# Gate rows of a two-block transformer kernel: summed over partitions on GpSimd instead of TensorE and VectorE

## The chip, the cores and the metric

The kernel runs on one core of a Trainium2 chip. The metric is device time of one execution in microseconds (us). The engines are called as the profile calls them: PE (TensorE, matrix products; PEld is its weight load), DVE (VectorE), ACT (ScalarE), POOL (GpSimd), SP (SyncE, which issues most DMAs). SBUF is the working memory of 128 partitions, PSUM the eight banks that PE writes.

## What is computed

Two transformer blocks run one after the other on 256 tokens of width 1024, in float32. The parts that matter here:

```python
# modulation, from a conditioning vector c of 1024 values
mod  = silu(c)   @ w_ada[l]   + b_ada[l]      # first block: 6 vectors of 1024 (sh1, sc1, gt1, sh2, sc2, gt2)
ada  = silu(c_2) @ w_ada_2[l] + b_ada_2[l]    # second block: 9 vectors of 1024
# first block
x = x + gt1 * mix(x, ctx)                                            # gate 0
x = x + gt2 * swiglu(modulate(rmsnorm(x), sh2, sc2), w_ffn_in, w_ffn_out)   # gate 1
x = rmsnorm(x, g_final)
# second block
x = x + 0.5 * g1 * swiglu(modulate(rmsnorm(x), sh1, sc1), ...)       # gate 2
x = x + g2 * (merged @ w_out)                                        # gate 3
x = x + 0.5 * g3 * swiglu(modulate(rmsnorm(x), sh3, sc3), ...)       # gate 4
x = rmsnorm(x, final_norm)
```

A gate is one vector of 1024 that multiplies every token's update. There are five of them. A swiglu is `(silu(h @ Wa) * (h @ Wb)) @ Wout` with inner width 2816.

## The kernel before

**Products in three parts.** Each weight tile of 1 MB (128 x 2048 floats, a "unit") is loaded by SP into one of three `raw` buffers. ACT rounds it to a high half (`whi`, line 862), DVE subtracts to get the low half (`wlo`, line 1912, a DVE operation with two SBUF inputs), and PE forms high x high, high x low and low x high (line 1291). PE may start a unit when its low half is ready (`lo_ready`). The activations have high and low halves in the same way: `A_both`, `B_hi`, `B_lo`.

**Stages.** The order on each engine is written out by hand, and engines meet only at semaphores. The stages are: the first block's mixer (units `P1`, from `dd` and `k` to `gla_out` and `mix_out`), `ffn(0)`, `ffn(1)`, the second block's mixer (`P2`, ending in `bra`, `brb`, `out2`), `ffn(2)`. Between them stands a norm. A feed-forward block has 11 pieces of 256 inner columns. Step i does two "up" units and one "down" unit. A step of PE waits for the DVE product of the piece before (`prod_done`) and its down product waits for `B_lo` (`flo_done`). `feed_forward_steps` (line 465) runs the steps, partly as a hardware loop of three steps a turn.

**Modulation.** The vectors `silu(c) @ w_ada` are not formed on PE. A unit of modulation is 256 columns: 1 MB of weights lands in `ada_raw`, and DVE adds eight products of a column block with a scalar per partition into `acc` (lines 1916 and 1920). After that each partition holds a part of the sum, and the sum over the 128 partitions is still to be taken. `GATE_UNITS` are the first of the four units of each gate. Gate r becomes a row `GR`, the same 1024 values in every partition, as follows:
- POOL loads the bias row into `GR` (`gate_bias`, line 716);
- PE multiplies a matrix of ones with `acc`, which sums over partitions and repeats the result in all of them (`gate`, line 1363): two products of 128x512, which in float32 are two passes each;
- DVE adds the two PSUM banks to `GR` (`gate_row`, line 1982).

Gate 0 is formed ahead of `mix_out`, gates 1, 2 and 4 ahead of the last down unit of the three feed-forward blocks, gate 3 ahead of `out2`. DVE then multiplies results with `GR`.

**POOL** otherwise issues the loads of modulation weights in the mixers (`load_ada`, line 776), computes the powers for the norms (`split_norm`, `piece_norm`, `twice_norm`), and turns a bias table around for the second block's attention (line 833). It works strictly in the order of its program.

**Modulation units of the last block.** Units 48 to 51, gate 4's, are loaded and summed in steps 0, 7, 8 and 9 of `ffn(2)` (`LAST_STEPS`). In `ffn(0)` and `ffn(1)` there is one such unit in every step from 0 to 9.

Of the kernel before, what the change touches and what calls it, by code (L numbers as in the profile page):

```python
# [15 lines left out]
P = 128  # L16
# [106 lines left out]
ADA_FFN = [n for n in range(len(ADA)) if NADA1 <= n < ADA_P2 or n >= ADA_LAST]  # L123
ADA_MIX = [n for n in range(len(ADA)) if n not in ADA_FFN]

LAST_STEPS = (0, NF - 4, NF - 3, NF - 2)


def ada_pos(n):
# [17 lines left out]
def build(nc, a, out):  # L147
    with ExitStack() as ctx:
# [3 lines left out]
        def sem(name):  # L152
            return ctx.enter_context(nc.semaphore(name))
# [182 lines left out]
        as_rows = sem("as_rows")  # L336
        as_turn = sem("as_turn")
        as_done = sem("as_done")
        gr_mm = sem("gr_mm")
        gr_done = sem("gr_done")  # L340
        x_ready = sem("x_ready")
        sq_done = sem("sq_done")
# [121 lines left out]

        def feed_forward_steps(eng, f, step):

            end = NF - 1 if f < 2 else NF - 4
            with eng.Fori(0, (end - 1) // 3) as j:
                for m in range(1, 4):
                    step((j, m), m)  # L470
            for i in range(end, NF - 1):
                step(i, i)


        def cview(w, c0, n=UC):
# [164 lines left out]

            return 7 if n in (3, 4) else 3

        def gate_bank(r):

            return {0: 6, 3: 2}.get(r, 4)

        def h_count(n, k):

# [54 lines left out]
        def _(pool):  # L703
# [12 lines left out]
            def gate_bias(r):  # L716
                blk, c0 = ADA[GATE_UNITS[r]]
                b = a["b_ada"] if blk == 0 else a["b_ada_2"]
                pool.dma_start(GR, b[0, c0:c0 + D].partition_broadcast(P)).then_inc(gr_in, 16)

            def negative_root(dst, src):

# [98 lines left out]
            for n in range(7, NADA1):  # L821
                load_ada(n)
                if n == 8:
                    pool.wait_ge(on_done, 8)
                    gate_bias(0)
            split_norm(2)
            gate_bias(1)
            twice_norm()
            gate_bias(2)
            pool.wait_ge(u_in, 16)  # L830
# [4 lines left out]
            for f in range(HR):  # L835
                ins = nc.gpsimd.memset(inv[:, f:f + 1], float(10000.0 ** (-2.0 * f / ROPE)))
            ins.then_inc(inv_done, 1)
            piece_norm(1, 8, rstd_done)
            gate_bias(3)
            load_ada(ADA_P2)  # L840
            for j, w in ((0, QR), (1, KVR)):
                pool.wait_ge(act_evac, EV2[j][1])
                root(rs2[:, 2 * j:2 * j + 2], ss2[:, 2 * j:2 * j + 2], w).then_inc(lat_rs, 1)
            for n in range(ADA_P2, ADA_LAST):
                if n > ADA_P2:
                    load_ada(n)
            split_norm(5)
            gate_bias(4)
            piece_norm(2, 14, frs_done)


# [437 lines left out]
        def _(pe):  # L1289
# [70 lines left out]
                            ins.then_inc(tr_done, 1)  # L1360
                keep_warm(warm, 3)

            def gate(r):

                g0 = GATE_UNITS[r]
                pe.wait_ge(*ada_done(g0 + 3))
                pe.wait_ge(gr_in, 16 * (r + 1))
                for x in range(2):
                    c = UC * ada_pos(g0) + 512 * x
                    ins = mm(bank[gate_bank(r) + x][:], ones[:], acc[:, c:c + 512], True, True)  # L1370
                ins.then_inc(gr_mm, 1)

            def shift_and_scale(n, b):

                pe.wait_ge(*ada_done(NORM_UNITS[n][1] + 3))
# [158 lines left out]
            def ffn(f):  # L1534
                u0, n0 = BASE_FFN[f], NF * f

                def up_step(u, b, half, k):

                    s = ring(u)
                    ws = slice(P * half, P * half + P)  # L1540
                    wh = whi[s][:].rearrange("p (k w) -> p k w", k=KD)[:, k, ws]
                    wl = wlo[s][:].rearrange("p (k w) -> p k w", k=KD)[:, k, ws]
                    o = bank[b + half]
                    pair = A_both[:, k, :, :].rearrange("p s t -> p (s t)")
                    if k:
                        mm(o[:, 0:T], wl, A_hi[:, k, :], False, False, skip_group_check=True)
                        return mm(o[:], wh, pair, False, k == KD - 1, skip_group_check=True)
                    mm(o[:], wh, pair, True, False, skip_group_check=True)
                    return mm(o[:, 0:T], wl, A_hi[:, k, :], False, False, skip_group_check=True)

                def up(u, i, b):

                    pe.wait_ge(lo_ready, lin(3, i, u + 1))
                    for half in range(2):
                        for k in range(KD):
                            ins = up_step(u, b, half, k)
                    ins.then_inc(unit_used, 1)

                def first_up(u, b, before):

                    for k in range(KD):
                        pe.wait_ge(hlo_done, before + k + 1)
                        for half in range(2):
                            ins = up_step(u, b, half, k)
                    ins.then_inc(unit_used, 1)

                def down(u, i, m, first, last):

                    pe.wait_ge(lo_ready, lin(3, i, u + 1))
                    pe.wait_ge(flo_done, lin(1, i, n0 + 1))  # L1570
                    s = ring(u)
                    wh = whi[s][:].rearrange("p (k w) -> p k w", k=2)
                    wl = wlo[s][:].rearrange("p (k w) -> p k w", k=2)
                    for t in range(TT):
                        for x in range(2):
                            for k in range(2):
                                ts, cs = slice(P * t, P * t + P), slice(512 * x, 512 * x + 512)
                                kb = 2 * (m % 3) + k
                                ins = three(bank[2 * t + x][:], (wh[:, k, cs], wl[:, k, cs]),
                                            (B_hi[:, kb, ts], B_lo[:, kb, ts]), False,  # L1580
                                            first and k == 0, last and k == 1, skip_group_check=True)
                            if last and 2 * t + x < 3:
                                ins.then_inc(bank_down, 1)
                    ins.then_inc(unit_used, 1)

                def step(i, m):
                    pe.wait_ge(prod_done, lin(1, i, n0 + 1))
                    up(u0 + 2, i, 4)
                    up(u0 + 3, i, 6)
                    down(u0 + 4, i, m, False, False)  # L1590


                pe.wait_ge(lo_ready, u0 + 1)
                first_up(u0, 0, low_count(2 + f + (f == 2)))
                up(u0 + 1, 0, 2)
                up(u0 + 2, 0, 4)
                up(u0 + 3, 0, 6)
                pe.wait_ge(prod_done, n0 + 1)
                down(u0 + 4, 0, 0, True, False)
                feed_forward_steps(pe, f, step)  # L1600
                pe.wait_ge(prod_done, n0 + NF)
                gate((1, 2, 4)[f])
                down(u0 + 2, NF - 1, NF - 1, False, True)

            def second():
# [52 lines left out]
                for n2, (kind, n) in enumerate(P2):  # L1658
                    u = BASE_P2 + n2
                    b = BANKS2[n2]  # L1660
                    s = ring(u)
                    if (kind, n) == ("out2", 0):
                        gate(3)
                    pe.wait_ge(lo_ready, u + 1)
                    wait_banks(n2, BEFORE2[n2][:1] if (kind, n) == ("bra", 0) else BEFORE2[n2], EV2)
                    if kind in ("uq", "ukv"):
# [190 lines left out]
            for u, (kind, n) in enumerate(P1):  # L1857
                if u < 2:
                    continue
                b = BANKS1[u]  # L1860
                if kind == "mix_out" and n == 0:
                    gate(0)
                pe.wait_ge(lo_ready, u + 1)
                wait_banks(u, BEFORE1[u], EV1)
                x = B if kind in ("conv_out", "gla_out") else A
# [37 lines left out]
        def _(dve):  # L1903
# [64 lines left out]
            def columns(n, b, gain, bias0, src):  # L1968
# [9 lines left out]
                    link(tt(by4(scale[:, s, :]), sums[:, 1], by4(bcol[:, bias0 + KD:bias0 + 2 * KD]), ALU.add))  # L1978
                    ins = stt(scale[:, s, :], scale[:, s, :], 1.0, vec[:, gain:gain + KD], ALU.add, ALU.mult)
                ins.then_inc(as_done, 1)  # L1980

            def gate_row(r):
                dve.wait_ge(gr_mm, r + 1)
                for x in range(2):
                    g = GR[:, 512 * x:512 * x + 512]
                    ins = tt(g, g, bank[gate_bank(r) + x][:], ALU.add)
                ins.then_inc(gr_done, 1)

            def norm(n):
                src, dst = (ctxX if n == 0 else xg if n == 3 else X), norm_source(n)  # L1990
# [314 lines left out]
            def ffn(f):  # L2305
# [41 lines left out]
                product(NF - 1, 4)  # L2347
                split(u0 + 3 * NF)
                low(NF - 1, NF - 1)
                r = (1, 2, 4)[f]  # L2350
                gate_row(r)
                dve.wait_ge(gr_done, r + 1)
                if f != 1:
                    dve.wait_ge(fin_in, 16 * (f // 2 + 1))
                for t in range(TT):
# [34 lines left out]
            def second():  # L2390
# [126 lines left out]
                for n2 in range(N2):  # L2517
# [31 lines left out]
                    if n2 in ADA2_STEP:  # L2549
                        adapt_half(ADA_P2 + ADA2_STEP.index(n2))  # L2550
                    if P2[n2] == ("out2", 0):
                        gate_row(3)
                        dve.wait_ge(gr_done, 4)
                evac2(N2 - 1)

# [11 lines left out]
            for u in range(N1):  # L2567
                if u:
                    evac1(u - 1)

                gla_step(2 * (u - 1 - U_Q) + 1)
                if u and u != U_V:
                    split(u + 2)
                gla_front(u)
                gla_step(2 * (u - U_Q))
                if u in (U_Q + 1, U_Q + 2):
                    decayed_queries(u - U_Q - 1)
                if P1[u - 1][0] == "ch":
                    conv(P1[u - 1][1])
                if P1[u - 2][0] == "ch":  # L2580
                    conv_low(P1[u - 2][1])
                if u == U_CB + 8:
                    norm_heads()
                if u in MOD_STEP:
                    n = MOD_STEP[u]
                    adapt(n, 0, acc[:, UC * ada_pos(n):UC * ada_pos(n) + UC], ADA[n][0])
                if P1[u] == ("mix_out", 0):
                    gate_row(0)
                    dve.wait_ge(gr_done, 1)
            evac1(N1 - 1)  # L2590
            norm(2)
# [59 lines left out]
```

## Time and profile before

| | |
|---|---|
| median of 3 runs | 1157.66 us (1157.28 to 1157.92) |
| span of the profiled execution | 1156.4 us |
| PE busy | 1118.4 us, 97% |
| DVE busy | 853.4 us, 74% |
| ACT busy | 571.7 us, 49% |
| POOL busy | 74.7 us, 6% |
| mean granted clock of PE | 0.991 |

The span runs from the first to the last instruction; the measured time is 1.26 us longer than it. In the rows, L1912 is line 1912 of the kernel, a shape `128x2048` is partitions x elements, and `arena` is one large SBUF tensor that holds most intermediate tiles, so `acc` and `GR` appear as `arena` and PSUM banks as `twin`. Times are us unless marked ns. A PE pass is recorded longer than the distance at which passes follow each other.

### The profile page before, as it was taken

What the parts mean: (1) busy time and instruction counts of PE and PEld (TensorE: products, weight loads), DVE (VectorE), ACT (ScalarE), POOL (GpSimd) and SP (SyncE); (2) the same over time, 40 slices, a digit from 0 to 9 for tenths busy, and PEclk for the clock granted to TensorE, in tenths of its full rate; (3) what the DMA queues carried; (4) which work ended last, traced back from release to release, by engine and by line L of the source; (5) the groups of instructions that cost most, each with busy time, mean ns of one, the idle gap of its engine ahead of it and who ended that gap; (6) DMA issues with size and microseconds to landing.
All of it is one profiled execution on the core that took longest, in us unless ns stands there. A gap on an engine that the chain in (4) does not pass through costs nothing.

```text
span 1156.4 us, 19131 instructions
## 1 busy us (share of the span) xinstructions
PE 1118.4 (97%) x7744; PEld 1008.5 (87%) x7744; DVE 853.4 (74%) x1082; ACT 571.7 (49%) x733; POOL 74.7 (6%) x143
## 2 busy tenths in 40 slices
PE   2999999999999999999999999999999999999997
PEld 2899988999999888888788888889999998888885
DVE  1578766897777688877888778878777776755676
ACT  3495434544434644445454454446655546444442
POOL 4000000100000100000200000011000001000001
PEclk8899999999999999999999999999999999999999
DMA  9934554688875488778468777747965654655771
GB/s 287 291 114 140 188 175 154 183 273 263 296 233 187 154 282 272 238 247 293 154 226 271 252 258 263 239 152 240 292 183 182 222 178 165 218 182 191 234 247 37
DMA packets 192548, 250.29 MB, mean 216 GB/s; under 512 B 4859, under 2 KB 171966, under 8 KB 192350
## 3 DMA queue, kind: packets, MB, share of 16 engines
q1 hardware_dynamic: 183838, 216.92, 57.8%
q0 software_dynamic: 8640, 32.38, 8.4%
q8 instruction: 51, 0.84, 0.3%
q14 instruction: 19, 0.16, 0.0%
HBM read 248.23 MB, written 1.05 MB: 216 GB/s over the span
## 4 chain that ended last, share of the span: by engine, by line
PE 87%; DVE 7%; ACT 2%; SPq 2%; DMA 1%; issue 1%; POOL 0%; POOLq 0%; DVEq 0%; ACTq 0%
PE twin L1291 85%; DVE wlo L1912 2%; DVE arena L1920 2%; DMA arena<-in_w_ada 1%; DVE arena L1912 1%; ACT arena L862 1%; DVE X L1912 1%; ACT whi L862 1%; PE twin L1628 1%; SPq L520 1%; SPq L570 0%; DVE arena L1916 0%; PE twin L1749 0%; PE twin L1416 0%; DVE B_lo L1912 0%
## 5 line engine op out<-in xcount | busy, mean ns | idle before, releaser
L1291 PE MATMUL twin<-A_both,whi 128*128 128x256 f32 (+1 forms) x2208 | 578.7, 339 | 3.1 <-DVE A_both L1912 1.6
L1912 DVE TENSOR_TENSOR wlo<-raw,whi 128x2048 fp32r<-128x2048 f32 (+1 forms) x171 | 386.9, 2263 | 117.1 <-ACT whi L862 117.0
L1291 PE MATMUL twin<-A_both,wlo 128*128 128x256 f32 x1632 | 436.5, 280 | 0.0
L862 ACT ACTIVATE whi<-raw 128x2048 fp32r<-128x2048 f32 x169 | 323.2, 1913 | 206.8 <-PE twin L1291 205.7
L1291 PEld LDWEIGHTS twin<-A_both,whi 128*128 128x128 f32 x2208 | 370.1, 190 | 46.1 <-issue 7.9
L1291 PEld LDWEIGHTS twin<-A_both,wlo 128*128 128x128 f32 x1632 | 309.2, 189 | 11.4 <-DVE A_both L1912 0.6
L1920 DVE SCALAR_TENSOR_TENSOR arena<-ada_raw,arena 128x256 f32<-128x256 f32 (+2 forms) x322 | 167.3, 520 | 15.9 <-issue 1.7
L862 ACT ACTIVATE arena<-twin 128x512 f32<-128x512 f32 (+5 forms) x171 | 90.8, 556 | 111.5 <-PE twin L1291 81.9
L862 ACT ACTIVATE arena<-arena 128x512 f32<-128x512 f32 (+7 forms) x132 | 69.9, 559 | 149.1 <-DVE arena L1912 116.0
L1291 PE MATMUL twin<-whi,B_hi 128*128 128x512 f32 (+2 forms) x340 | 126.6, 372 | 0.2 <-DVE B_lo L1912 0.2
L1291 PE MATMUL twin<-wlo,B_hi 128*128 128x512 f32 (+2 forms) x340 | 125.1, 368 | 0.0
L1291 PE MATMUL twin<-whi,B_lo 128*128 128x512 f32 (+2 forms) x340 | 125.1, 368 | 0.0
L1291 PE MATMUL twin<-whi,A_both 128*128 128x256 f32 x640 | 117.3, 285 | 0.4 <-DVE A_both L1912 0.4
L1912 DVE TENSOR_TENSOR arena<-arena,twin 128x512 f32<-128x512 f32 x92 | 62.5, 683 | 62.3 <-ACT arena L862 48.0
L1291 PEld LDWEIGHTS twin<-whi,A_both 128*128 128x128 f32 x640 | 99.8, 192 | 1.7 <-issue 1.5
L1291 PE MATMUL twin<-wlo,A_both 128*128 128x256 f32 x320 | 90.5, 283 | 0.0
L1291 PEld LDWEIGHTS twin<-whi,B_lo 128*128 128x128 f32 x340 | 64.1, 189 | 11.3 <-issue 0.7
L1291 PEld LDWEIGHTS twin<-wlo,B_hi 128*128 128x128 f32 x340 | 64.1, 189 | 10.7
L1291 PEld LDWEIGHTS twin<-whi,B_hi 128*128 128x128 f32 x340 | 64.1, 189 | 10.2 <-issue 1.1
L1291 PE MATMUL twin<-B_hi,whi 128*128 128x256 f32 x224 | 64.1, 286 | 1.1 <-DVE B_lo L1912 1.1
L1291 PE MATMUL twin<-arena 128*128 128x64 f32 (+9 forms) x528 | 63.9, 303 | 0.1
L1291 PE MATMUL twin<-B_lo,whi 128*128 128x256 f32 x224 | 63.6, 284 | 0.0
(137 smaller groups left out, 900.6 us busy)
## 6 DMA issues: line engine op xcount, KB each, us to landing
raw<-in_w_in SPq DMA_DIRECT2D x48, 1024.0 KB, 5.7
raw<-in_ffn_w_in SPq DMA_DIRECT2D x44, 1024.0 KB, 5.1
ada_raw<-in_w_ada POOLq DMA_DIRECT2D x28, 1024.0 KB, 6.0
ada_raw<-in_w_ada SPq DMA_DIRECT2D x24, 1024.0 KB, 5.4
raw<-in_w_ffn_in SPq DMA_DIRECT2D x22, 1024.0 KB, 5.1
raw<-in_ffn_w_out SPq DMA_DIRECT2D x22, 1024.0 KB, 5.0
raw<-in_w_ffn_out SPq DMA_DIRECT2D x11, 1024.0 KB, 5.0
arena<-in_w_ada SPq DMA_DIRECT2D x8, 1024.0 KB, 11.8
```

Of the source, the lines that this page charges most:

```text
L520: sp.dma_start(dst, src).then_inc(landed[ring(u)], 16)
L862: return nc.scalar.activation(o, i, f, **kw)
L1291: return nc.tensor.matmul(o, l, r, start=start, stop=stop, **kw)
L1628: ins = nc.tensor.transpose(bank[7][:, P * c:P * c + P], Pb[j % 2][:, P * c:P * c + P], ident)
L1912: return nc.vector.tensor_tensor(o, x, y, op)
L1920: return nc.vector.scalar_tensor_tensor(out=o, in0=x, scalar=sc, in1=y, op0=op0, op1=op1)
```

## The change

The sum over partitions of a gate moves to POOL, which reduces `acc` over partitions into `GR` with one instruction (`partition_all_reduce`), then adds the bias row in a second. The bias row is loaded into a free part of `acc` (`gate_add`), since `GR` is now the reduction's output. PE's gate products, DVE's additions and the semaphore `gr_mm` go. DVE waits for `gr_done` where it used to add. The units of gate 4 move to steps 0 to 3 of `ffn(2)`, and there the steps 1 to 3 are written out and the loop covers 4 to 9, instead of a loop over 1 to 6 and 7 to 9 written out. On POOL, the first modulation load of the second mixer now stands ahead of gate 3's bias load.

```diff
-LAST_STEPS = (0, NF - 4, NF - 3, NF - 2)
+LAST_STEPS = (0, 1, 2, 3)
...
         def feed_forward_steps(eng, f, step):
 
-            end = NF - 1 if f < 2 else NF - 4
-            with eng.Fori(0, (end - 1) // 3) as j:
-                for m in range(1, 4):
+            first = 1 if f < 2 else 4
+            for i in range(1, first):
+                step(i, i)
+            with eng.Fori(0, (NF - 1 - first) // 3) as j:
+                for m in range(first, first + 3):
                     step((j, m), m)
-            for i in range(end, NF - 1):
-                step(i, i)
...
-        def gate_bank(r):
-
-            return {0: 6, 3: 2}.get(r, 4)
+        def gate_add(r):
+
+            return at(0 if r == 2 else 16, D)
...
-                pool.dma_start(GR, b[0, c0:c0 + D].partition_broadcast(P)).then_inc(gr_in, 16)
+                if r:
+                    pool.wait_ge(as_mm, min(r, 3))
+                pool.dma_start(gate_add(r), b[0, c0:c0 + D].partition_broadcast(P)).then_inc(gr_in, 16)
+
+            def gate_row(r):
+
+                g0 = GATE_UNITS[r]
+                c = UC * ada_pos(g0)
+                pool.wait_ge(*ada_done(g0 + 3))
+                link(nc.gpsimd.partition_all_reduce(GR, acc[:, c:c + D], P, bass.bass_isa.ReduceOp.add))
+                pool.wait_ge(gr_in, 16 * (r + 1))
+                nc.gpsimd.tensor_tensor(GR, GR, gate_add(r), ALU.add).then_inc(gr_done, 1)
...
                     gate_bias(0)
+            gate_row(0)
             split_norm(2)
             gate_bias(1)
+            gate_row(1)
             twice_norm()
             gate_bias(2)
...
             ins.then_inc(inv_done, 1)
+            gate_row(2)
             piece_norm(1, 8, rstd_done)
+            load_ada(ADA_P2)
             gate_bias(3)
-            load_ada(ADA_P2)
...
                     load_ada(n)
+            gate_row(3)
             split_norm(5)
             gate_bias(4)
+            gate_row(4)
             piece_norm(2, 14, frs_done)
...
-            def gate(r):
-
-                g0 = GATE_UNITS[r]
-                pe.wait_ge(*ada_done(g0 + 3))
-                pe.wait_ge(gr_in, 16 * (r + 1))
-                for x in range(2):
-                    c = UC * ada_pos(g0) + 512 * x
-                    ins = mm(bank[gate_bank(r) + x][:], ones[:], acc[:, c:c + 512], True, True)
-                ins.then_inc(gr_mm, 1)
...
                 pe.wait_ge(prod_done, n0 + NF)
-                gate((1, 2, 4)[f])
                 down(u0 + 2, NF - 1, NF - 1, False, True)
...
-            def gate_row(r):
-                dve.wait_ge(gr_mm, r + 1)
-                for x in range(2):
-                    g = GR[:, 512 * x:512 * x + 512]
-                    ins = tt(g, g, bank[gate_bank(r) + x][:], ALU.add)
-                ins.then_inc(gr_done, 1)
...
-                r = (1, 2, 4)[f]
-                gate_row(r)
-                dve.wait_ge(gr_done, r + 1)
+                dve.wait_ge(gr_done, (1, 2, 4)[f] + 1)
```

The calls `gate(0)` ahead of `mix_out` and `gate(3)` ahead of `out2` on PE, and `gate_row(0)` and `gate_row(3)` on DVE, are removed in the same way; the waits for `gr_done` stay.

On POOL, around the end of the first mixer, before (the DMAs into `ada_raw` are the modulation loads, the DMA from `in_b_ada` is a gate's bias):

```order
L719 DMA arena<-in_b_ada 128x1024 [waits on_done]
L783 DMA ada_raw<-in_w_ada 128x8x256 [waits ada_mac] x7
L737 TENSOR_SCALAR arena<-arena 128x2 [waits part_done]
L742 TENSOR_TENSOR arena<-arena 128x1 [waits sq_done,pool_chain]
L723 TENSOR_TENSOR arena<-arena 128x1 [waits pool_chain]
```

The same place now:

```order
L720 DMA arena<-in_b_ada 128x1024 [waits on_done]
L793 DMA ada_raw<-in_w_ada 128x8x256 [waits ada_mac] x7
L727 ISA
L727 ISA arena<-arena 128x1024 [waits ada_mac]
L729 ISA
L729 TENSOR_TENSOR arena<-arena 128x1024 [waits gr_in,pool_chain]
L747 TENSOR_SCALAR arena<-arena 128x2 [waits part_done]
```

Four rows come between the last modulation load and the norm's first operation: the reduction, the addition, and ahead of each a row without operands. The same four rows stand at the other four places.

On DVE, the start of `mix_out`, before (the first row is the low half of the merged activations, the second the low half of a weight unit):

```order
L1912 TENSOR_TENSOR A_both<-arena,A_both 128x2x256 [waits mghi_done]
L1912 TENSOR_TENSOR wlo<-raw,whi 128x2048 [waits hi_ready]
L1912 TENSOR_TENSOR arena<-arena,twin 128x512 [waits gr_mm]
L1912 TENSOR_TENSOR arena<-arena,twin 128x512
L1912 TENSOR_TENSOR arena<-twin,arena 128x512 [waits unit_used,gr_done]
L1912 TENSOR_TENSOR X<-arena 128x2x256 [waits xr_in,dve_evac]
```

The same place now:

```order
L1912 TENSOR_TENSOR A_both<-arena,A_both 128x2x256 [waits mghi_done]
L1912 TENSOR_TENSOR wlo<-raw,whi 128x2048 [waits hi_ready]
L1912 TENSOR_TENSOR arena<-twin,arena 128x512 [waits unit_used,gr_done]
L1912 TENSOR_TENSOR X<-arena 128x2x256 [waits xr_in,dve_evac]
L1912 TENSOR_TENSOR wlo<-raw,whi 128x2048 [waits hi_ready]
```

The two additions with the wait for PE of 128x512 into `arena` from `twin` are gone, and the wait for the gate row stands on the first use of it, as it did.

## Rows read from the trace of the kernel before

**Rows 1.** The page: busy time of each engine, and the chain that ended last.

```profile
PE 1118.4 (97%) x7744; PEld 1008.5 (87%) x7744; DVE 853.4 (74%) x1082; ACT 571.7 (49%) x733; POOL 74.7 (6%) x143
...
PE 87%; DVE 7%; ACT 2%; SPq 2%; DMA 1%; issue 1%; POOL 0%; POOLq 0%; DVEq 0%; ACTq 0%
```

**Rows 2.** Tile of ones (ns min/median/max), then PE's timeline (start, us) at four gates.

```profile
L1291 PE MATMUL twin<-arena,ones x52: 590/592/617, 354.1 to 1141.7; 128*32 128x512 f32 x32, 128*128 128x512 f32 x20
...
354.02 0.28 PE L1291 MATMUL twin<-B_hi,wlo 128*128 128x256 f32 x1
354.15 1.88 PE L1291 MATMUL twin<-arena,ones 128*128 128x512 f32 x4
...
563.45 1.88 PE L1291 MATMUL twin<-arena,ones 128*128 128x512 f32 x4
...
931.08 1.88 PE L1291 MATMUL twin<-arena,ones 128*128 128x512 f32 x4
...
1140.45 1.88 PE L1291 MATMUL twin<-arena,ones 128*128 128x512 f32 x4
```

**Rows 3.** DVE's timeline around the gates: last low halves, and additions.

```profile
358.06 0.69 DVE L1912 TENSOR_TENSOR A_both<-arena,A_both 128x512 fp32r<-128x512 f32 x1 [0.76 <-ACT A_both L862]
...
362.07 1.28 DVE L1912 TENSOR_TENSOR arena<-arena,twin 128x512 f32<-128x512 f32 x2
...
563.18 0.68 DVE L1912 TENSOR_TENSOR B_lo<-arena,B_hi 128x512 fp32r<-128x512 f32 x1
...
935.82 0.69 DVE L1912 TENSOR_TENSOR A_both<-arena,A_both 128x512 fp32r<-128x512 f32 x1 [0.70 <-ACT A_both L862]
...
939.84 1.28 DVE L1912 TENSOR_TENSOR arena<-arena,twin 128x512 f32<-128x512 f32 x2
...
1138.34 0.69 DVE L1912 TENSOR_TENSOR B_lo<-arena,B_hi 128x512 fp32r<-128x512 f32 x1 [0.70 <-ACT B_hi L862]
```

**Rows 4.** POOL's timeline: what stands ahead of rows 0 to 3.

```profile
323.88 0.89 POOL L783 DMA_DIRECT2D ada_raw<-in_w_ada  x1 [11.93 <-DVE arena L1920]
...
381.85 0.95 POOL L719 DMA_DIRECT2D arena<-in_b_ada  x1
...
720.43 0.59 POOL L836 MEMSET arena<- 128x1 f32 x16
...
903.64 0.75 POOL L783 DMA_DIRECT2D ada_raw<-in_w_ada  x1 [8.14 <-DVE arena L1920]
```

**Rows 5.** POOL by line and form; the landing of POOL's bias loads.

```profile
L833 POOL COPY arena<-arena 128x256 f32<-128x256 f32 x8 | 5.4, 676 | 134.1 <-DVE wlo L1912 134.1
...
DMA to landing us min/median/max: 3.8/5.5/8.6
```

**Rows 6.** Timelines of POOL and DVE from 781 to 788 us.

```profile
783.22 1.07 POOL L713 TENSOR_SCALAR arena<-arena 128x2 f32<-128x2 f32 x1 [12.53 <-ACT arena L862]
...
785.86 1.45 POOL L713 TENSOR_SCALAR arena<-arena 128x2 f32<-128x2 f32 x1 [0.76 <-ACT arena L862]
...
781.96 2.29 DVE L1912 TENSOR_TENSOR wlo<-raw,whi 128x2048 fp32r<-128x2048 f32 x1 [2.22 <-ACT whi L862]
784.97 2.29 DVE L1912 TENSOR_TENSOR wlo<-raw,whi 128x2048 fp32r<-128x2048 f32 x1 [0.72 <-ACT whi L862]
```

**Rows 7.** Timelines of DVE and PE where rows 0, 2 and 3 fall.

```profile
331.01 3.61 DVE L1920 SCALAR_TENSOR_TENSOR arena<-ada_raw,arena 128x256 f32<-128x256 f32 x7
...
337.35 0.68 DVE L1912 TENSOR_TENSOR arena<-twin,arena 128x512 f32<-128x512 f32 x1
...
738.23 0.69 DVE L1912 TENSOR_TENSOR arena<-arena 128x512 f32<-128x512 f32 x1
...
741.58 0.39 PE L1291 MATMUL twin<-wlo,B_hi 128*128 128x512 f32 x1
...
918.66 1.29 DVE L1912 TENSOR_TENSOR B_lo<-twin,B_hi 128x512 fp32r<-128x512 f32 x2 [0.42 <-ACT B_hi L862]
...
919.50 0.35 PE L1291 MATMUL twin<-B_hi,whi 128*128 128x256 f32 x1 [1.06 <-DVE B_lo L1912]
```

More of the change, by code:

```diff
@@ L338, in build @@
         as_done = sem("as_done")
-        gr_mm = sem("gr_mm")
         gr_done = sem("gr_done")
@@ L1661, in second @@
                     s = ring(u)
-                    if (kind, n) == ("out2", 0):
-                        gate(3)
                     pe.wait_ge(lo_ready, u + 1)
@@ L1860, in _ @@
                 b = BANKS1[u]
-                if kind == "mix_out" and n == 0:
-                    gate(0)
                 pe.wait_ge(lo_ready, u + 1)
@@ L2551, in second @@
                     if P2[n2] == ("out2", 0):
-                        gate_row(3)
                         dve.wait_ge(gr_done, 4)
@@ L2587, in _ @@
                 if P1[u] == ("mix_out", 0):
-                    gate_row(0)
                     dve.wait_ge(gr_done, 1)
```

## The prediction, made blind

> **What bounds the kernel now.** I read the page first. PE is busy 97% of the span and holds 87% of the chain that ended last; POOL is busy 6% [rows 1]. So PE time that goes is worth its length, POOL time is free while nobody waits, and DVE (74%) counts only where PE, or the chain after PE's last product, waits for it. Then the lines of the tile of ones (the gate products), the timelines of PE, DVE and POOL around the five gates, and last the places where POOL would read SBUF for long.
>
> **What is removed.** Each gate is four passes of 128x512 on PE: 0.59 us each, four in 1.88, so they start (1.88 - 0.59) / 3 = 0.43 apart and keep PE 1.72 us [rows 2]. What comes back depends on what PE would wait for instead:
> - Gate 0. mix_out's first unit takes the low halves in four quarters of 12 products, 0.12 us apart [rows 2], 1.44 a quarter. Started at 354.15 instead of 355.87 it wants the last low half at 358.47, and DVE has it at 358.75 [rows 3]. Gain 1.4.
> - Gates 1 and 2. The last down product of a feed-forward block waits for B_lo, ready at 563.18 + 0.68 = 563.86, about 0.45 after PE is free at 563.45 [rows 2, 3]. Gain 1.25 each (the second block ends alike).
> - Gate 3. Low halves again: the last is there at 935.82 + 0.69 = 936.51, wanted at 931.08 + 4.32 = 935.40 [rows 2, 3]. PE waits 1.15 of the 1.72. Gain 0.55.
> - Gate 4. B_lo is there at 1139.03, PE is free at 1140.45 [rows 2, 3]. Gain 1.7.
>
> The ten DVE additions (1.28 us a pair) go as well [rows 3]. In the blocks' ends they stand beside PE's last product, at gates 0 and 3 beside mix_out's or out2's first unit: nothing of their own. Gains: 1.4 + 1.25 + 1.25 + 0.55 + 1.7 = 6.15 us.
>
> **What is added, on POOL.** Five times: a row without operands, the reduction of 128x1024, again a row without operands, an addition of 128x1024. No row shows any of them. The bare rows I take for changes of POOL's code, one to the reduction's set and one back. Below they cost nothing; above, the longest landing of POOL's DMAs, 8.6 us [rows 5]. I take 7, since code must arrive in the same way (median 5.5) and then start. The reduction: a copy of 256 elements takes 0.67 us, so one pass over 1024 takes 2.7 [rows 5]; below it is one pass, above seven (128 partitions halved seven times), 19 us. I take the value nearer the copy, two and a half passes (in, across, out), 6.7 us. The addition: one to two copies, 2.7 to 5.4; I take 3. One gate row is then 7 + 6.7 + 7 + 3 = 24 us.
>
> The Trainium skill ("GPSIMD Engine Reference", 2.1 Instruction dispatch) puts the first call of freshly loaded code at about 6 us; by that two changes would be 12 us, an estimate, and a gate row 22. No row here shows it.
>
> **Who waits for it.** Row 0 stands behind POOL's last modulation load of that stage, free at 324.8: done at 348.5, wanted by DVE at 363.4, where the addition of 362.07 ended [rows 3, 4]. Row 1: from 382.8, wanted past 563. Row 2: behind the memsets, 721.0 to 745, wanted at the block's end, one step (three units) after 741.8. Row 3: behind the last load, 904.4 to 928, wanted at 941 [rows 3, 4]. Row 4 needs the last block's units. With these in steps 0 to 3 it is ready some 110 us early; in the old steps it would not be. The moved units cost nothing: the first two blocks have such a unit in every step, the last has them in four, and PE keeps the same pace in all of them. SP issues the three loads six steps earlier, behind that step's weights as in the other blocks. Queued behind each row on POOL are norms (piece_norm after rows 2 and 4, split_norm after rows 0 and 3), and all are due later than the row. So by waits alone nothing is late, with 13 us to spare at the tightest.
>
> **What the rows hide.** POOL and DVE meet at SBUF. A POOL operation on two elements started at 783.22 and ended at 784.30, where DVE's low half (781.96 + 2.29 = 784.25) ended; the next started at 785.86 and ended at 787.31, DVE's at 787.26 [rows 6]. Twice an instruction of a fraction of a us stood until the DVE operation with two SBUF inputs was over. If the two exclude each other, a POOL operation that reads for 6.7 us stops every such DVE operation, the low halves and modulation sums, and what is queued behind. In before no POOL operation reads long enough to show that direction; its cost is bounded by 0 and by the whole reduction, and I take the whole, since the direction that is shown is held to the end.
>
> The skill's "SBUF — State Buffer", section "Who interferes with whom", says it: a DVE instruction with two SBUF inputs contends with a GpSimd instruction that reads SBUF, and whoever issues first keeps the shared pair for the whole instruction. The rows above agree for DVE ahead of POOL. By it the sum is the one below; without it, rival A's.
>
> Place by place, with 6.7 us held:
> - Row 0: POOL reads from about 332, between two sums of the chain that starts at 331.01. The evacuation of 337.35 ends at 344.7 instead of 338.0 [rows 7]. PE's third gla_out unit needs its bank; A unit is 48 products 0.12 apart, 5.76, and the fourth ended at 354.15, so PE is at the third at 342.6 [rows 2]. Stall 2.1. Of the lag DVE makes up about 1 us a unit (74% busy), 3.5 units to the last low half, and the addition's hold puts one back: low half at 363.0, wanted at 360.6. Stall 2.3. Together 4.4.
> - Row 1: at the start of a block, either side of a low half. Allowance 1.2, between 0 and row 2's.
> - Row 2: read from 729.6, behind a low half. The block's product of 738.23 + 0.69 comes 5.2 later (1.5 of DVE's idle time taken up), at 744.1; PE wants it at 741.8 [rows 7]. Stall 2.3.
> - Row 3: read at 911.5, ahead of the low half whose followers end in B_lo at 918.66. PE already waits 1.06 for that B_lo [rows 7], so a delay of 5 is a stall of 5.0.
> - Row 4: starts when step 3's sums are done, so it meets that step's product. Some 4 late, 2 to 3 spare [as in rows 7]. Stall 1.7.
>
> Losses 14.6, gains 6.15, net +8.45: 1156.4 + 8.45 = 1164.9 span. The execution shown spans 1156.4 and the median is 1157.66, so 1.3 lies around it: 1166.1.
>
> **Rivals.**
> A, the DVE isn't held: POOL works unseen. For it: 6% busy, 13 us to spare; and DVE is only seen to hold POOL, never the reverse. Against: rows 6. 1157.7 - 6.15 = 1151.5.
> B, held in pieces: the reduction lets DVE in between its parts, so each hold is about a third. Losses near 6, gains 6: 1157.5.
> C, late rows: beyond 36.7 us a row, row 3 comes after DVE wants it. DVE queues out2's residual and the low halves of the next units behind that wait, and PE stops. It needs code changes of over 13 us each; at 15, 3 us late at row 3 and 1 at row 0. With the holds 1170.
> D, the reduction is slow as a whole. The same skill page, 3.2 Cross-partition, measures a partition reduction of 128x2048 at 247.7 us; half of it, 124, would be an estimate for this one. From rows, the seven passes of 19 us are the limit: a row of 36 us, just inside, but each hold three times as long: about 1195. By the page's figure rows 0, 2 and 3 would each be some 105 late, near 1450. No row speaks for either.
>
> **Chances.** Forecast (whole hold) 0.50; A 0.30; B 0.13, split over the three signs; C 0.04; D 0.03. A measurement of this kernel tells 0.2% (2.3 us) from no change. Faster: A and 0.03 of B, 0.33. Same: 0.07 of B and 0.03 of the forecast's low end, 0.10. Slower 0.57. The forecast's own range, with holds of 4 to 8 us, is 1159 to 1172. The range for 8 in 10 has to reach A as well: 1151 to 1172.
>
> **What would show it.** In the new profile: no gate products, last down products at once behind B_lo; five POOL reductions of 5 to 9 us with gaps of 5 to 9 around them. Right: DVE operations with two SBUF inputs that record 6 to 9 us instead of 2.29 or 0.49 beside them, and PE idle 2 to 5 us at the third gla_out unit and before the branch b products. Wrong: those DVE operations keep their 2.29 us, PE has no new gaps, and the end is 6 us earlier.

## The result: 14.6 us slower

| | before | after |
|---|---|---|
| median, runs of one chip | 1157.49 us (1157.28 to 1157.92) | 1172.11 us (1171.71 to 1176.50) |
| span of the profiled execution | 1156.4 us | 1170.2 us |
| ratio to before | | 1.0133, 95% 1.0121 to 1.0146 |

The forecast was 1166.1, with a range to 1172; the median lies at the upper end, a tenth of a microsecond past it. The sign was right; the loss was 14.6 us where 8.5 were forecast.

### The profile page after: what moved, and what is told of

It reads as the page before. It is cut to its first block, busy times and chain, and to the rows that moved or that the text cites. A ratio compares the mean times of both kernels' runs of the same rounds, so it can differ in the third digit from the quotient of the medians.

```text
span 1170.2 us, 19111 instructions
## 1 busy us (share of the span) xinstructions
PE 1116.5 (95%) x7724; PEld 1009.2 (86%) x7724; DVE 868.5 (74%) x1072; ACT 571.7 (49%) x733; POOL 124.3 (11%) x153
## 4 chain that ended last, share of the span: by engine, by line
PE 77%; DVE 12%; ACT 4%; issue 3%; DMA 2%; SPq 2%; POOL 0%; POOLq 0%; DVEq 0%; ACTq 0%
PE twin L1306 75%; DVE arena L1920 4%; DVE wlo L1912 3%; DVE arena L1912 2%; ACT whi L877 2%; DMA ada_raw<-in_w_ada 1%; ACT arena L877 1%; DMA arena<-in_w_ada 1%; DVE arena L1916 1%; DVE X L1912 1%; PE twin L1632 1%; SPq L519 1%; DVE A_both L1912 0%; ACT A_both L877 0%; SPq L569 0%
## 5 line engine op out<-in xcount | busy, mean ns | idle before, releaser
L1912 DVE TENSOR_TENSOR wlo<-raw,whi 128x2048 fp32r<-128x2048 f32 (+1 forms) x171 | 392.3, 2295 | 112.7 <-ACT whi L877 112.4
L1920 DVE SCALAR_TENSOR_TENSOR arena<-ada_raw,arena 128x256 f32<-128x256 f32 (+2 forms) x322 | 173.5, 539 | 15.9 <-issue 1.7
L1912 DVE TENSOR_TENSOR arena<-arena,twin 128x512 f32<-128x512 f32 x82 | 56.1, 684 | 55.9 <-ACT arena L877 48.0
L1306 PE MATMUL twin<-B_hi,wlo 128*128 128x256 f32 x224 | 64.1, 286 | 0.0
```

Of the source, the lines that this page charges most:

```text
L1306: return nc.tensor.matmul(o, l, r, start=start, stop=stop, **kw)
L1912: return nc.vector.tensor_tensor(o, x, y, op)
L1920: return nc.vector.scalar_tensor_tensor(out=o, in0=x, scalar=sc, in1=y, op0=op0, op1=op1)
```

## The profile after

From the profile's page of the changed kernel. PE has 20 matrix products fewer and is busy 95% instead of 97% [rows 1]; DVE executes ten operations fewer and is still busy 15 us longer, and its part of the chain that ended last rose from 7% to 12%.

```profile
PE 1116.5 (95%) x7724; PEld 1009.2 (86%) x7724; DVE 868.5 (74%) x1072; ACT 571.7 (49%) x733; POOL 124.3 (11%) x153
...
PE 77%; DVE 12%; ACT 4%; issue 3%; DMA 2%; SPq 2%; POOL 0%; POOLq 0%; DVEq 0%; ACTq 0%
```

POOL by line and form (busy us, mean ns, idle before), then its timeline at rows 0, 2 and 3.

```profile
L727 POOL PARTITION_ALL_REDUCE arena<-arena x5 | 36.3, 7250 | 107.2 <-DVE arena L1920 82.1 <-issue 25.1
...
L729 POOL TENSOR_TENSOR arena<-arena 128x1024 f32<-128x1024 f32 x5 | 13.0, 2610 | 37.2 <-issue 37.2
...
332.13 6.25 POOL L727 PARTITION_ALL_REDUCE arena<-arena  x1 [9.27 <-DVE arena L1920]
345.94 3.39 POOL L729 TENSOR_TENSOR arena<-arena 128x1024 f32<-128x1024 f32 x1 [7.56 <-issue]
...
734.15 7.59 POOL L727 PARTITION_ALL_REDUCE arena<-arena  x1 [6.99 <-issue]
748.64 2.33 POOL L729 TENSOR_TENSOR arena<-arena 128x1024 f32<-128x1024 f32 x1 [6.91 <-issue]
...
926.42 6.13 POOL L727 PARTITION_ALL_REDUCE arena<-arena  x1 [10.53 <-issue]
940.29 2.40 POOL L729 TENSOR_TENSOR arena<-arena 128x1024 f32<-128x1024 f32 x1 [7.74 <-issue]
```

A gate row costs POOL what was worked out for it: 7.0 to 10.5 us of idle time ahead of a reduction (row 0's 9.3 hold a wait for the last sum as well) and 6.9 to 7.7 ahead of an addition, 6.1 us of reduction (up to 8.2 where it first waits for DVE), 2.4 us of addition. The idle times stand where the bare rows without operands stand in POOL's order; that POOL changes its code in them is my reading, the trace shows only the time. Row 0 ended at 349.3 and was wanted 18 us later. No row is late.

DVE beside them. Alone, a sum of 128x256 takes 0.49 us (seven in 3.61, [rows 7]), the first of a chain 0.35, a low half 2.29, a 128x512 operation 0.69.

```profile
330.34 7.76 DVE L1920 SCALAR_TENSOR_TENSOR arena<-ada_raw,arena 128x256 f32<-128x256 f32 x7
...
347.72 2.16 DVE L1912 TENSOR_TENSOR arena<-arena,X 128x512 f32<-128x512 f32 x1
...
735.66 4.63 DVE L1916 TENSOR_SCALAR arena<-ada_raw,arena 128x256 f32 x1
...
748.64 2.89 DVE L1912 TENSOR_TENSOR arena<-arena 128x512 f32<-128x512 f32 x1
...
926.29 1.28 DVE L1912 TENSOR_TENSOR arena<-twin,arena 128x512 f32<-128x512 f32 x2
927.49 5.61 DVE L1912 TENSOR_TENSOR wlo<-raw,whi 128x2048 fp32r<-128x2048 f32 x1
```

Beside the reductions one operation is longer by 4.15 (7.76 - 3.61), 4.28 (4.63 - 0.35) and 3.32 (5.61 - 2.29). Beside the additions, 1.47 (2.16 - 0.69) and 2.20 (2.89 - 0.69). The two operations at 926.29 have one input in PSUM and one in SBUF and keep their 0.64 each beside the start of the reduction. From the start of the reduction, or from the end of the DVE operation that it waits for, DVE is held 4.2 to 4.4 us: not the whole reduction. The addition holds it for nearly its whole length.

PE's idle times of over 1.1 us behind the start-up, and the clock granted to it. The second fence has the columns length, busy time of PE, PEld, DVE, ACT and POOL (count), PEclk, DMA share, GB/s.

```profile
355.44 0.48 PE L1306 MATMUL twin<-whi,A_both 128*128 128x256 f32 x2 [1.62 <-DVE wlo L1912]
363.74 0.50 PE L1306 MATMUL twin<-whi,A_both 128*128 128x256 f32 x2 [3.75 <-DVE A_both L1912]
...
420.98 0.49 PE L1306 MATMUL twin<-A_both,whi 128*128 128x512 f32 x1 [2.38 <-DVE arena L1912]
...
751.66 0.79 PE L1306 MATMUL twin<-A_both,whi 128*128 128x512 f32 x1 [3.57 <-DVE arena L1912]
...
933.85 0.36 PE L1306 MATMUL twin<-B_hi,whi 128*128 128x256 f32 x1 [4.22 <-DVE B_lo L1912]
```

```profile
355.00:363.00 8.00, 4.55 (x36) 4.37 (x36) 5.31 (x7) 3.10 (x4) 0.00 (x0) 1.00 0.50 158
363.00:372.00 9.00, 8.26 (x56) 8.26 (x57) 6.47 (x5) 3.68 (x2) 0.00 (x0) 0.81 0.65 215
...
752.00:758.00 6.00, 6.00 (x22) 5.11 (x22) 5.89 (x7) 2.00 (x2) 0.00 (x0) 0.56 0.53 152
...
933.00:942.00 9.00, 8.15 (x55) 8.19 (x56) 6.70 (x9) 0.57 (x1) 1.71 (x1) 0.81 0.73 233
```

Behind each of the three longest idle times PE runs part of a stretch at 1.2 GHz instead of 2.4 (a granted clock, PEclk, of 0.5). In the kernel before it was at full clock at all three places. A stretch of 9 us at a mean of 0.81 has lost 1.7 us of pace, the 6 us at 0.56 have lost 2.6: some 6 us in all, and the prediction had no term for it.

By place, as the difference of the two traces at the ends of PE's units: row 0 with gate 0 +6.75 (3.0 forecast), row 1 +2.0 (1.2), row 2 +6.4 (2.3), row 3 +4.65 (5.0), row 4 nothing (1.7); gates 1 to 4 gave back 1.1, 1.45, 0.45 and 1.8. The start-up came out 1.6 shorter in this execution. That sums to 13.4, the spans differ by 13.8. In row 0 the forecast's stall of 2.1 at the third gla_out unit was 0.7; the loss came at mix_out, with the waits of 1.62 and 3.75 us.

## The experiments

The theory: POOL's reads hold DVE, DVE makes PE wait, and PE runs at half clock behind a long wait. The rivals are named with each run. In all, before was 1157.55 to 1157.67 us.

**The moved units alone.** The kernel before, with gate 4's units in steps 0 to 3, the loop over the steps as in the changed kernel, and nothing else.

```diff
-LAST_STEPS = (0, NF - 4, NF - 3, NF - 2)
+LAST_STEPS = (0, 1, 2, 3)
...
```

> The kernel before with one part of the change: gate 4's units in steps 0 to 3 of the last block. Gates stay on PE and DVE. My account (prices of the changed kernel come from POOL's reads alone): same as before, 1157.5 within 1.5 us. Rival (the three extra sums in a row in steps 1 to 3, or their loads beside the block's first weights, cost PE time): 1159 to 1162, with new PE idle time in the last block's steps 1 to 3.

1157.24 us, ratio 0.9997 (0.9987 to 1.0006). They cost nothing, as the prediction had it.

**The gates' work taken away.** From the kernel before, with nothing in its place.

```diff
-                gate((1, 2, 4)[f])
...
-                gate_row(r)
-                dve.wait_ge(gr_done, r + 1)
+                dve.wait_ge(gr_in, 16 * ((1, 2, 4)[f] + 1))
```

> The kernel before without the ten gate products on PE and the ten additions on DVE, and nothing on POOL in their place; it leaves out the sums of the gates, so that a gate is its bias row only. It measures the gain by itself. By the steps of the prediction 6.15 us less: 1151.3, shared as 1.4, 1.25, 1.25, 0.55 and 1.7 over gates 0 to 4. Rival (each of the five gates takes the 1.88 us that it keeps PE, no wait takes its place): 1148. Rival (the gates were hidden, and the changed kernel lost less than it seems): 1156 or more.

1152.68 us, ratio 0.9955 (0.9938 to 0.9971): 5.0 us instead of 6.15. By place 0.2, 1.1, 1.1, 0.4 and 1.8. Only gate 0 differs, 0.2 against 1.4: its low halves came 0.35 us later in this execution, and PE, 0.8 earlier from the start-up, stood 1.3 us for them. In the next run gate 0 gave 1.2.

**The same row on POOL, with 64 of 1024 columns.** It tells the code changes from the reads.

```diff
-                link(nc.gpsimd.partition_all_reduce(GR, acc[:, c:c + D], ...))
+                link(nc.gpsimd.partition_all_reduce(gate_add(r)[:, 0:64], acc[:, c:c + 64], ...))
...
-                nc.gpsimd.tensor_tensor(GR, GR, gate_add(r), ALU.add)
+                nc.gpsimd.tensor_tensor(GR[:, 0:64], GR[:, 0:64], gate_add(r)[:, 0:64], ALU.add)
```

> The changed kernel with the reduction and the addition over 64 of the 1024 columns; it leaves out the sums of the other 960 columns of each gate. All ten code changes of POOL, the order and the waits stay; what goes is the length of POOL's reads. If the reads held DVE (my account), DVE has no operation of over 3 us beside POOL's, PE has no idle time over 1.1 us in the middle, its clock doesn't fall, and the time is 1151 to 1153. If the code changes or their transfers were what disturbed, or the order of POOL's program, it stays at 1168 to 1172.

1152.26 us, ratio 0.9956 (0.9939 to 0.9972). POOL's and PE's timelines of this kernel:

```profile
332.74 0.78 POOL L727 PARTITION_ALL_REDUCE arena<-arena  x1 [8.60 <-DVE arena L1920]
340.29 0.31 POOL L729 TENSOR_TENSOR arena<-arena 128x64 f32<-128x64 f32 x1 [6.76 <-issue]
...
358.16 0.51 PE L1306 MATMUL twin<-whi,A_both 128*128 128x256 f32 x2 [0.24 <-DVE A_both L1912]
```

All ten code changes are there at their full length (6.8 to 9.6 us), no DVE operation takes over 2.34 us, and the time is that of the kernel without any gate work. So the code changes and POOL's order cost nothing; the length of what POOL reads and writes costs all of the difference to the changed kernel, 1172.1 - 1152.3 = 19.8 us. This kernel doesn't tell the reads from the writes, which became shorter too, and its bias row lands in GR, as before the change. The reads are the likelier part: the two operations at 926.29 write SBUF as well and were not held, nor was one of that kind in the middle of a hold (620.03, three rows on POOL, below).

**Without the addition.** The bias is left out.

```diff
-                link(nc.gpsimd.partition_all_reduce(GR, acc[:, c:c + D], ...))
                 pool.wait_ge(gr_in, 16 * (r + 1))
-                nc.gpsimd.tensor_tensor(GR, GR, gate_add(r), ALU.add).then_inc(gr_done, 1)
+                nc.gpsimd.partition_all_reduce(GR, acc[:, c:c + D], ...).then_inc(gr_done, 1)
```

> The changed kernel without POOL's addition of the bias rows (the bias is left out of the gates). The reduction of 128x1024 stays. My account: the addition held DVE as well, 1.5 us at mix_out's low halves in row 0 and 2.2 us on the product of the block in row 2, and with PE's half clock behind these stalls it was worth some 5 us: 1167, and the idle time at 751.66 (3.57 us) falls to about 1.4 with no fall of the clock there, the one at 363.74 to about 2. Rival (the addition holds nothing that anyone waits for, all of it is the reduction): 1171 to 1172.

1165.57 us, ratio 1.0073 (1.0056 to 1.0089). The idle times of its PE that answer to those above:

```profile
362.20 0.50 PE L1305 MATMUL twin<-whi,A_both 128*128 128x256 f32 x2 [3.77 <-DVE A_both L1911]
...
745.90 0.49 PE L1305 MATMUL twin<-A_both,whi 128*128 128x512 f32 x1 [1.37 <-DVE arena L1911]
...
926.40 0.52 PE L1305 MATMUL twin<-B_hi,whi 128*128 128x256 f32 x1 [4.04 <-DVE B_lo L1911]
```

So the 19.8 us are 13.3 of the reduction (1165.6 - 1152.3) and 6.5 of the addition (1172.1 - 1165.6), with the pace behind each; the four runs of this kernel lie within 2.6 us. Row 2 is as expected, 1.37 and full clock; with 0.75 more at the block's end it costs 2.4, the forecast's 2.3. Row 1 has no idle time of 0.9 us or more: its 2.4 in the changed kernel was the addition's. In row 0 the last wait kept its 3.8 us against my 2; there only the wait ahead of it (1.6) went, and the clock fell behind the 3.8 us as before.

**PE kept busy where it waited.** Products of no use ahead of two waits of the changed kernel: `keep_warm(bank, n)` issues n products of ones by ones into a PSUM bank.

```diff
+                if low is mglo_done and before == 0:
+                    pe.wait_ge(gr_in, 16)
+                    keep_warm(6, 14)
...
+                                if m == 0 and n == 0 and k == 0 and not kk:
+                                    keep_warm(7, 16)
```

> The changed kernel with products of ones by ones (128x128, results unused) on PE where it stood idle with the clock at half afterwards: 14 of them (3.1 us) ahead of mix_out's first low halves, 16 (3.6 us) ahead of the first product of branch b. Both fit into the idle times there, 3.76 and 4.22 us. If PE's clock falls because PE had been idle, the granted clock stays at full speed behind both places and the time is the two losses of pace less, 1.7 + 1.5 us: 1169. Rival (the clock falls there for another reason, as the load that POOL's reduction puts on the chip, or the pace is no part of the loss): 1172, with 0.5 still shown at 364.8 and 934.8.

1172.7 us (1170.0 to 1175.4), ratio 1.0121 (1.0104 to 1.0138): by the time, inconclusive. I had put the second filler ahead of branch a's products, two units before the wait, which is in branch b: PE arrived 3.5 us later there and then waited 1.07 instead of 4.22. And rows 1 and 2 met other DVE operations in this execution (PE idle 3.1 and half clock at 422). Its stretches:

```profile
357.00:365.00 8.00, 7.68 (x64) 7.50 (x64) 5.31 (x7) 3.42 (x4) 0.00 (x0) 1.00 0.54 173
...
933.00:942.00 9.00, 7.93 (x67) 7.72 (x66) 8.87 (x8) 3.54 (x4) 3.03 (x1) 1.00 0.44 149
421.00:428.00 7.00, 5.96 (x19) 5.10 (x20) 6.55 (x7) 3.58 (x3) 0.00 (x0) 0.51 0.82 262
```

At both filled places the clock stayed full, at the second with the reduction beside it; where PE stood idle for 3.1 us it fell. Two kernels without any reduction, below, settle it.

**In quarters.**

```diff
+                for q in range(4):
+                    s = slice(256 * q, 256 * q + 256)
+                    link(nc.gpsimd.partition_all_reduce(GR[:, s], acc[:, c + 256 * q:c + 256 * q + 256], ...))
...
+                for q in range(4):
+                    s = slice(256 * q, 256 * q + 256)
+                    ins = nc.gpsimd.tensor_tensor(GR[:, s], GR[:, s], gate_add(r)[:, s], ALU.add)
```

> The changed kernel with each reduction in four of 128x256, one waiting for the other, and each addition in four of 128x256. The same values are read, with gaps in between in which DVE can start. My account (DVE is held by one POOL instruction at a time, so one long hold becomes four short ones with an operation of DVE between): no DVE operation is over its usual time by more than 1.5 us, PE's idle times over 3 us fall under 2 us, no half clock, and the time is 1155 to 1161. Rival (DVE gets no turn between, or a small reduction takes nearly as long as a large one, so that the holds add up to more): 1170 to 1185.

1163.34 us, ratio 1.0053 (1.0036 to 1.0069): between the two ranges, and a miss for both. POOL and DVE at row 0 of this kernel, PE at row 0 and at the end of the second block, and the stretch behind that:

```profile
332.55 9.14 POOL L729 PARTITION_ALL_REDUCE arena<-arena  x4 [9.13 <-DVE arena L1926]
...
334.96 3.18 DVE L1918 TENSOR_TENSOR wlo<-raw,whi 128x2048 fp32r<-128x2048 f32 x1
...
360.22 0.51 PE L1312 MATMUL twin<-whi,A_both 128*128 128x256 f32 x2 [3.02 <-DVE A_both L1918]
...
763.96 0.52 PE L1312 MATMUL twin<-whi,B_hi 128*128 128x512 f32 x1 [2.74 <-DVE B_lo L1918]
...
763.00:769.00 6.00, 5.04 (x15) 4.05 (x16) 2.62 (x5) 0.95 (x3) 0.00 (x1) 0.72 0.61 175
```

DVE does get its turn between the parts: the low half is longer by 0.9, not by 4. At row 3 PE waits for B_lo no longer than in the kernel before. But the low halves of row 0 are the end of a chain without slack: four holds of 0.2 to 0.9 us add up in it, and there the pieces bring 0.7 us of idle time (3.75 to 3.02). And the loss of row 2 moves to the block's end: PE waits 2.74 us for the last B_lo, and the clock falls there as it does behind the 3.02 us. By place the pieces lose 4.3 (without gate 0's 1.2), 1.4, 4.5 and 0.9 us at rows 0 to 3, two of the stalls with half clock behind them, which I had not expected.

**Two rows moved.** All five still on POOL; rows 1 and 2 begin right behind a modulation sum in the middle of a block, as row 4 did.

```diff
-                pool.wait_ge(*ada_done(g0 + 3))
+                pool.wait_ge(*ada_done(19 if r == 1 else g0 + 3))
...
             gate_bias(2)
+            gate_row(2)
             pool.wait_ge(u_in, 16)
...
-            gate_row(2)
```

> The changed kernel with two rows moved in POOL's program, everything else the same. Row 1 waits for unit 19 of the modulation instead of unit 15 (from the start of the first feed-forward block to its step 3), row 2 stands ahead of the eight copies of the bias table, so that it runs in step 1 of the second block, right behind unit 27's sums. Both then begin where row 4 began, behind a sum, and row 4 cost PE nothing. If the place decides, rows 1 and 2 cost nothing either: 2.0 and 6.4 us less, 1163.7, and PE's idle times at 420.98 and 751.66 are gone. Rival (row 4 was harmless because the last block has fewer sums for DVE, not because of the place; a block with a sum in every step has no room for a hold): 2 to 4 us at each of the new places, 1168 to 1172.

1164.57 us, ratio 1.0060 (1.0043 to 1.0077). PE's idle times at rows 1 and 2 are gone; by place they gave back 2.0 and 6.3 us. The medians differ by 7.5; in the traces the start-up came out 1.5 longer and row 0 1.0 shorter than in the changed kernel's. The place decides, not the load of the block.

**Rows 1, 2 and 4 on POOL at these places, gates 0 and 3 on PE as before.** Cuts of the edit, against the kernel with the moved rows.

```diff
-            gate_row(0)
...
-            gate_row(3)
...
+                if kind == "mix_out" and n == 0:
+                    gate(0)
...
+                    if (kind, n) == ("out2", 0):
+                        gate(3)
```

> As the kernel with the moved rows 1 and 2, but gates 0 and 3 are formed on PE and DVE as before; POOL forms rows 1, 2 and 4. Gates 1, 2 and 4 each gave back 1.1, 1.1 and 1.8 us where nothing was lost. If rows 1, 2 and 4 cost nothing at these places: before less 3.95, 1153.7. Rival (the holds cost 2 to 4 us each at the new places of rows 1 and 2): 1158 to 1161. This is also the version that should beat both kernels.

1153.89 us (1153.35 to 1154.62), ratio 0.9967 (0.9956 to 0.9979): 3.7 us faster than before, 18 faster than the changed kernel. POOL and DVE at row 2 of this kernel:

```profile
616.19 8.06 POOL L732 PARTITION_ALL_REDUCE arena<-arena  x1 [37.66 <-DVE arena L1937]
...
615.97 2.29 DVE L1929 TENSOR_TENSOR wlo<-raw,whi 128x2048 fp32r<-128x2048 f32 x1
618.17 0.68 DVE L1929 TENSOR_TENSOR arena<-arena,twin 128x512 f32<-128x512 f32 x1
620.03 0.69 DVE L1929 TENSOR_TENSOR arena<-arena,twin 128x512 f32<-128x512 f32 x1 [1.19 <-ACT arena L880]
620.76 2.44 DVE L1929 TENSOR_TENSOR arena<-arena 128x512 f32<-128x512 f32 x1
```

Here is why the place is harmless. The reduction waits until the low half ends at 618.2, and two operations that read PSUM and an idle 1.2 us of DVE fall into its hold. Only the product behind them is late, by 1.75 us, and a block has that to spare. All of row 2 costs this kernel 0.4 us at most.

**The clock by itself.** The kernel before with five additions of no use on DVE ahead of mix_out's last low half, without and with filler products ahead of gate 0.

```diff
+                if P1[u] == ("gla_out", 3):
+                    for _ in range(5):
+                        link(tt(at(16, D), X[:, 0, :], X[:, 0, :], ALU.add))
...
+                    pe.wait_ge(gr_in, 16)     # this and the next line in the second kernel alone
+                    keep_warm(6, 18)
                     gate(0)
```

> The kernel before with five additions of 128x1024 (about 1.2 us each, results unused) on DVE behind its work for the last gla_out unit, and no reduction on POOL. They delay the last low half that mix_out waits for by some 6 us: it comes at 364.9, PE is through three quarters at 360.2, so PE stands idle some 4.7 us. If an idle PE alone brings the clock down, 0.5 is shown behind this idle time for 3.4 us, and the time is 4.7 + 1.7 more: 1164. Rival (the half clock of the changed kernel came with POOL's reductions, not with PE's idle time): full clock, 1162.3.

> As the kernel with the stall, and 18 products of ones by ones (128x128, some 4.0 us) on PE ahead of gate 0's. The last low half comes at the same time and sets when mix_out's first unit ends, but PE now stands idle only 0.7 us before it. If the idle time brings the clock down, it stays at full speed and the time is 1.7 us less than with the bare stall: 1162.3. Rival: no difference.

1165.80 us (ratio 1.0065, 1.0052 to 1.0079) and 1162.78 us (1.0042, 1.0028 to 1.0055). The bare stall is longer than the 4.7 us that I had expected. PE of the bare stall, then of the filled one:

```profile
366.05 0.80 PE L1291 MATMUL twin<-whi,A_both 128*128 128x256 f32 x2 [6.10 <-DVE A_both L1912]
...
366.00:372.00 6.00, 5.95 (x33) 5.95 (x34) 4.83 (x6) 2.98 (x2) 0.00 (x0) 0.62 0.23 67
```

```profile
365.19 0.51 PE L1291 MATMUL twin<-whi,A_both 128*128 128x256 f32 x2 [1.19 <-DVE A_both L1914]
...
366.00:372.00 6.00, 6.00 (x52) 6.00 (x51) 5.68 (x6) 2.13 (x2) 0.00 (x0) 1.00 0.33 115
```

POOL forms no gate row here, and the clock falls all the same: PE's idle time alone brings it down. The filled kernel is 3.0 us faster. Of these 0.9 are the last low half, which came earlier in its execution (365.19 against 366.05); the other 2.1 are pace, and the row says 2.3 (6 us at a mean of 0.62). The Trainium skill ("TensorE: Matmul & The Clock Gate", Terms) prices the time below full clock at half its length. The traces agree: the mean of 0.62 is 4.6 us of the 6 at half clock, by that rule an estimate of 2.3 us, and without the low half's 0.9 the two kernels differ by 2.1.

## Why the prediction was off

- **The gains (6.15).** Measured 5.4 (narrow rows) and 5.0 (no work). Gates 1 to 4 within 0.2. Gate 0 gave 1.2 in one kernel and 0.2 in the other, by when the last low half came; the 1.4 of the forecast was its upper end.
- **POOL's row (24 us), nothing late.** Right in that nothing is late, and near in its parts: changes of up to 10.5 us instead of 7, a reduction of 6.1 instead of 6.7, an addition of 2.4 instead of 3. The moved units at nothing were right too.
- **The hold.** The mechanism was right, and it was the step on which the rivals turned: A (no hold) is excluded by DVE operations that are 4 us longer and by the narrow rows; C and D by rows that end in time and a reduction of 6 us. The length was 4.4, not 6.7: the last 1.7 us of the reduction don't hold. B's idea, DVE let in between the parts of one reduction, is not what happened. Cutting the reduction makes B, but not B's price: 1163.3, not 1157.5.
- **The step that failed: the losses, 14.6 against 19.8.** One term was sized wrong and one was missing. The first is the addition: priced at 1 us in row 0 alone, it cost 6.5. It holds DVE nearly as long as it lasts, and it comes 14 us behind the start of the reduction, where I looked at no timeline; in row 2 it began in the same ten nanoseconds as the block's product. The second is PE's pace: each stall was taken at its length, and behind three of them PE ran at half clock. That cost some 6 us. The two overlap: the 2.6 us of pace at row 2 went with the addition, so they belong to its 6.5. The other 3.4 hid a third error, that of the hold's length: the reduction, forecast at 13.6, came to 13.3 with shorter holds and a slower clock, which is luck.
- **Row by row.** Row 3, where the read stands straight ahead of what PE waits for, came out near (5.0 against 4.65), but by luck: the wait grew by 3.2 us (1.06 to 4.22) where 5.0 were forecast, and the slower clock cost some 1.7 on top. Rows 0 and 2 lost 8.0 (6.75 and the gain of gate 0) and 6.4 where 4.4 and 2.3 were forecast. Row 4's loss was forecast and didn't come: I let it meet the product with 1.7 to pay, and the product had the time to spare.

The Trainium skill ("SBUF — State Buffer", Who interferes with whom) is borne out in who is held: operations with two SBUF inputs, and the TENSOR_SCALAR with one at 735.66, a kind that the page lists among those that can contend, but not those with one input in PSUM. Where it says that the pair is kept for the whole instruction, the trace shows 4.4 of 6.1 us for the reduction; the measurement decides.

Open: why the last 1.7 us of a reduction don't hold (a reading part and a writing part would fit, nothing here shows it), and how much of the spread of the changed kernel (1170 to 1176 in its forms with whole rows) comes from which DVE operation a row happens to meet.

## What to carry to other kernels

Work that moves to POOL can be free of waits and still not free: list each of its SBUF reads with its length, lay it over DVE's timeline, and count what it holds of those DVE operations that read SBUF alone; then move the read to where DVE idles or reads PSUM. Look at every instruction of the new work, the short last one as well. A long stall of PE can cost more than its length, as those of 2.7 to 6.1 us did here: look at the granted clock behind it.

## What was not expected of the hardware

- A reduction of 128x1024 over partitions takes 6.1 us, one of 128x256 1.8 and one of 128x64 0.78, all without a wait; it holds DVE for 4.2 to 4.4 of the 6.1.
- POOL takes some 7 to 10 us for each change between the reduction and ordinary operations, ten times in this kernel, and the time was not longer for it: 1152.3 us with all ten and narrow rows, 1152.7 without any.
- PE's clock stayed full behind an idle time of 2.38 us (420.98 in the changed kernel), but in the kernel with the moved rows a stretch with idle times of 1.75 (356.06) and 2.28 us (364.36) has a mean of 0.73. The length of one idle time doesn't tell it alone. The stretch, in the columns above:

```profile
356.00:366.00 10.00, 7.67 (x43) 7.49 (x44) 6.24 (x7) 4.86 (x4) 0.00 (x0) 0.73 0.63 211
```
